# The head of a streaming encoder kernel: order of the first loads and splits, and two sums on another engine

## The reference

```
def _swiglu(u, w_in, w_out):
    h = u @ w_in
    a, b = h[..., :D_FF], h[..., D_FF:]
    return (jax.nn.silu(a) * b) @ w_out

x = x + 0.5 * _swiglu(_rmsnorm(x, norm_ffn1[i]), ffn1_w_in[i], ffn1_w_out[i])
```

## Time and profile before

| | us |
|---|---|
| median of 3 runs | 1879.09 |
| lowest and highest run | 1878.52, 1880.51 |
| profiled execution, its own time | 1879.91 |
| its span, first to last instruction | 1878.1 |
| TensorE busy | 1855.2 (99%) |
| VectorE busy | 1251.5 (67%) |
| ScalarE busy | 866.9 (46%) |
| GpSimd busy | 329.5 (18%) |

### The profile page before, as it was taken

The page is one execution under the profiler, slowest core; times in us unless marked ns, Lnnn a source line. Parts: engine busy times, 40 slices in busy tenths (PEclk is TensorE's granted clock), DMA queues, the critical chain, the costliest instruction groups (busy, mean ns, idle before and its releaser), DMA issues.

```text
span 1878.1 us, 34441 instructions
## 1 busy us (share of the span) xinstructions
PE 1855.2 (99%) x13850; PEld 1834.6 (98%) x13850; DVE 1251.5 (67%) x1999; ACT 866.9 (46%) x1518; POOL 329.5 (18%) x352
## 2 busy tenths in 40 slices
PE   8999999999999999999999999999999999999998
PEld 8999999998999999999999999999989999999998
DVE  7874487668884488679853886563546888548853
ACT  7552355347552355346532553232334665235532
POOL 2220122131220122132201221300010322012112
PEclk9999999999999999999999999999999999999999
DMA  8773576334763576347644763231113576357632
GB/s 207 166 149 105 128 167 148 108 85 95 166 147 108 127 167 150 107 107 165 146 131 102 171 141 101 86 102 68 57 45 103 117 169 152 108 120 167 135 93 82
DMA packets 116830, 234.71 MB, mean 125 GB/s; under 512 B 13184, under 2 KB 15248, under 8 KB 116672
## 3 DMA queue, kind: packets, MB, share of 16 engines
q1 hardware_dynamic: 77440, 160.59, 28.7%
q0 software_dynamic: 38208, 69.42, 22.5%
q10 hardware_dynamic: 1024, 2.49, 0.4%
HBM read 228.92 MB, written 3.53 MB: 124 GB/s over the span
## 4 chain that ended last, share of the span: by engine, by line
PE 93%; DVE 4%; ACT 2%; DMA 1%; issue 1%; DVEq 0%; ACTq 0%
PE ps L1850 49%; PE ps L1840 39%; DVE w_lo L1231 1%; PE ps L1895 1%; PE ps L2167 1%; PE ps L2233 0%; DVE u L1285 0%; DMA raw_z<-in_ffn_in 0%; PE ps L2170 0%; DMA x<-in_x 0%; PE ps L2032 0%; PE ps L2157 0%; DVE rstd L1302 0%; ACT w_hi L726 0%; PE ps L2142 0%
## 5 line engine op out<-in xcount | busy, mean ns | idle before, releaser
L1850 PE MATMUL ps<-u,w_hi 128*128 128x288 f32 x4928 | 984.0, 295 | 11.7 <-DVE w_lo L1231 4.5
L1850 PEld LDWEIGHTS ps<-u,w_hi 128*128 128x128 f32 x4928 | 790.6, 188 | 16.4 <-DVE w_lo L1231 9.4
L1850 PE MATMUL ps<-u,w_lo 128*128 128x288 f32 x2464 | 727.1, 295 | 0.0
L1850 PEld LDWEIGHTS ps<-u,w_lo 128*128 128x128 f32 x2464 | 462.6, 188 | 0.0
L1840 PE MATMUL ps<-h_hi,w_hi 128*128 128x288 f32 x1386 | 294.4, 293 | 0.0
L1840 PE MATMUL ps<-h_lo,w_hi 128*128 128x288 f32 x1386 | 294.3, 293 | 0.0
L1840 PE MATMUL ps<-h_hi,w_lo 128*128 128x288 f32 x1386 | 294.3, 293 | 0.0
L726 ACT ACTIVATE w_hi<-w_raw 128x768 fp32r<-128x768 f32 (+3 forms) x164 | 136.0, 836 | 316.6 <-PE ps L1840 240.2
L1231 DVE TENSOR_TENSOR w_lo<-w_raw,w_hi 128x768 fp32r<-128x768 f32 (+3 forms) x164 | 168.8, 1038 | 160.6 <-ACT w_hi L726 158.4
L1840 PEld LDWEIGHTS ps<-h_hi,w_lo 128*128 128x128 f32 x1386 | 220.4, 188 | 0.0
L1840 PEld LDWEIGHTS ps<-h_hi,w_hi 128*128 128x128 f32 x1386 | 220.3, 188 | 0.0
(11 more groups left out here) (268 smaller groups left out, 2123.5 us busy)
## 6 DMA issues: line engine op xcount, KB each, us to landing
raw_a<-in_ffn_in SPq DMA_DIRECT2D x132, 256.0 KB, 4.2
w_raw<-in_ffn_out SPq DMA_DIRECT2D x64, 384.0 KB, 3.2
raw_y<-in_ffn_in SPq DMA_DIRECT2D x88, 256.0 KB, 3.6
raw_x<-in_ffn_in SPq DMA_DIRECT2D x88, 256.0 KB, 2.7
raw_x<-in_ffn_in POOLq DMA_DIRECT2D x88, 256.0 KB, 6.5
raw_y<-in_ffn_in POOLq DMA_DIRECT2D x88, 256.0 KB, 4.9
raw_z<-in_ffn_in POOLq DMA_DIRECT2D x88, 256.0 KB, 5.1
w_raw<-in_ffn_out SPq DMA_DIRECT2D x64, 320.0 KB, 3.0
```

The lines of the kernel that those rows point to most:

```text
L1850: mm = pe.matmul(dst, w, m, start=prod in ("M1", "M2", "M5") and kp == 0 and p == 0, stop=kp == KP - 1 and p == 2, skip_group_check=prod i ...
```

## The change

Five things change, all at the program's head. SyncE loads A21 of pair 1 ahead of x tile 1. SyncE waits for the landing of S1 of pair 0 before it issues A12, A12 and A22. ScalarE and VectorE split u7's part 0 of tile pair 1 before they read tile pair 2, and M5's block of pair 0 before all odd tiles. S2 of pairs 0 and 1 is made by a GpSimd add (`first_s2`), no longer by VectorE. And since VectorE's add no longer stands behind M5's `w_lo`, SyncE's loads of A21 for pairs 2 and 3 wait for that `w_lo` too.

```
@@ SyncE
                 if g >= 2:
                     sp.wait_ge(s2_summed, g - 1)
+                if 2 <= g < 4:
+                    sp.wait_ge(lo_split, f.unit(ph, "M5", n - 2) + 1)
...
             load_x(6)
+            load_a21(ffn_a, 0, 1)
             load_x(1)
-            load_a21(ffn_a, 0, 1)
...
             load_x(7)
+            sp.wait_ge(s1_summed[0], 16)
             load_ffn(ffn_a, ffn_b)
@@ GpSimd
+            def first_s2(n):
+
+                pool.wait_ge(a11_landed[n], 16)
+                pool.wait_ge(s1_summed[n], 16)
+                pool.tensor_tensor(raw_z[n][:, :], raw_y[n][:, :], raw_x[n][:, :], ALU.add).then_inc(s2_summed, 1)
+
             add_s1_first(ffn_a, 0)
-            add_s3_first(ffn_a, 0)
+            for n in range(2):
+                first_s2(n)
+                add_s3(ffn_a, 0, n)
@@ ScalarE; VectorE has the same moves with u7_low
+            u7_high(ffn_a, 1, 0)
             first_even(2)
-            u7_high(ffn_a, 1, 0)
...
+            upto(ffn_a.unit(0, "M5", 0))
             first_odd(0)
             first_odd(1)
-            upto(ffn_a.unit(0, "M5", 0))
@@ VectorE, in lo(u)
-                if SLOT[u] is None and prod == "M5":
+                if SLOT[u] is None and prod == "M5" and g >= 2:
```

More of the change, by code:

```diff
@@ L1446, in _ @@
             first_even(1)
+            u7_low(ffn_a, 1, 0)
             first_even(2)
-            u7_low(ffn_a, 1, 0)
             first_even(3)
```

## The result

Thirteen runs of each kernel on one chip: before 1878.78 us in the median (1875.51 to 1882.94), changed 1884.47 (1879.88 to 1888.07). The ratio is 1.0025 with a 95% interval of 1.0015 to 1.0034: the changed kernel is 4.7 us slower (2.8 to 6.4). The profiled execution of the changed kernel has a span of 1881.9 us, 1878.1 before. Of all runs told of here one, of the kernel before, was in a slower state (2589.94 us), and it is in no ratio.

What follows compares the result with a forecast made beforehand. TensorE was taken as the bound, with VectorE feeding it at the head; later M5 of pair 1 and slow clock put M2's end at 29.45 against 26.95, 2.5 us on 1879.09: 1881.6 us, range 1877.8 to 1884.2.

Steps and rivals of the forecast that it cites:

- L: Landing of GpSimd's accumulate making raw_x0 (S1 of pair 0): 14.8 us instead of 15.24, with bounds 12.0 and 15.24.
- if L is under 14: Sign for the changed kernel's profile: the forecast is wrong if that accumulate lands before 14 us.
- M1: Even tiles reordered at the head: no gain at M1's end, 14.46 us, and no effect on the clock.
- The first hole: TensorE's idleness before M5 of pair 0: w_lo held by GpSimd's add, start at L + 2.15 = 16.95, 0.7 us sooner.
- The second hole: TensorE idle between M5 of pairs 0 and 1 for 2.2 to 3.5 us, ending at 22.05 against 20.5.
- the second add: GpSimd's add from L + 2.5 to L + 3.8, costing VectorE some 0.9 us; bounds 0 and 1.3.
- The clock: TensorE at 0.50 for 5.9 us after 22.05, so M2 ends at 29.45 against 26.95, 2.5 us later.
- So the 2.5 us go through: From M2's end to the program's end: the 2.5 us delay carries through in full.
- nor does other work end later than TensorE: Premise after M2: M6's third quarter split and its matmul both move by some 2 us.
- rival B: Clock does not fall, or returns at once: -0.1 to +1.3 us, 1879.0 to 1880.4; chance 0.20.
- C: Rival at the head: the accumulate lands early, L = 12.0 to 13.5; 1877.2 to 1878.9 us; chance 0.13.
- D: Rival: held loads free nothing, L stays 15.2, second add costs 1.3; 2.0 to 4.6 us later; chance 0.22.

Runs made afterwards that it cites:

- the repetitions: The changed kernel, unchanged, compared twice more with the kernel before: ratios 1.0014 and 1.0013.
- loads only: The kernel before with only the loads' part: A21 of pair 1 ahead of x tile 1, A12, A12, A22 held back; ratio 1.0003.
- GpSimd's sums only: The kernel before with only S2 of pairs 0 and 1 made by GpSimd adds, loads and order as before; ratio 1.0005.
- swapped and filled: The kernel before with VectorE's M5 w_lo of pair 0 and next sum ahead of kp 1's odd split, plus seven small TensorE products before M5; ratio 1.0015.
- the filled kernel: The changed kernel with ten small unread TensorE products between M5 of pair 0 and M5 of pair 1; ratio 1.0014 to the kernel before.

## Why the prediction was right, and where it was not

**The time.** 2.5 us later was forecast, 4.7 (2.8 to 6.4) came first, 2.6 (0.6 to 4.7) and 2.4 (0.0 to 5.1) in the repetitions. The sign was right, and the size is that of the head in the profiles. By the first ratio more was lost than the head explains; the last section says where such differences can come from.

**L.** Forecast 14.8, measured 13.89, 13.89 and 13.49. The landing took 6.87, 6.46 and 6.64 us from the issue; forecast were 6.9 to 7.0, 0.45 less than before, and 0.5 to 1.1 less than the 7.4 and 7.5 of before came. The issue itself was at 7.02, 7.43 and 6.85, where I had kept 7.84. It is no gift of the change: the other four kernels with the changed loads have it at 6.96 to 8.09, so this is spread that one profile doesn't show. By my own sign, "if L is under 14", this term was wrong in all three, and the prediction came through by the term that cancelled it.

**M1.** Its end was forecast at 14.46, and the clock put at nothing. It ended at 15.16, 14.10 and 14.32: in the first profile the clock was at 0.50 from 11 to 14 us. That cost nothing, since M5's w_lo ended only at 15.86, but a part of the first hole was closed by it and not by M5. It isn't the new order's work: the clock fell in M1 in eight of the 14 profiles, three of them with the even tiles in the old order (loads only, GpSimd's sums only, swapped and filled).

**The first hole.** M5's w_lo was held by GpSimd's add and took 1.29 us (forecast 1.3 to 1.4), and TensorE started at L + 2.03 (forecast L + 2.15). At 15.92 for 16.95, this difference is L's.

**The second hole.** M5 of pair 1 starts at 22.05, the number forecast, by two errors that cancel: L 0.9 sooner, and L + 8.16 for L + 7.25. The term that was mis-sized is the second add, 0.9 with bounds of 0 and 1.3; the held split took 2.53 us for 0.76, 1.8 more. I had the split under way end before the add takes effect. It had begun 0.33 us ahead of the add, and ended 0.61 behind it. So the number 22.05 is luck; what it hangs on, VectorE's w_lo of pair 1 behind a held operation, is as forecast. My upper bound, one whole add of 1.3, left out that the add itself could be longer (1.59) and that the operation had most of its own time still before it when the add was over.

**The clock.** It fell in the second hole and stayed low for 5.8 us after work began, 5.9 forecast, so that M2's end at 29.68 met the 29.45 forecast. In the two others M2 ended 1.1 and 1.5 us sooner. The 5.9 us that I carried over from one row of the profile before were one draw, and that the first profile drew nearly the same was luck: the kernel before itself had 2.9 us in its second profile. The difference between the kernels hangs less on it than each time does: P is 2.73 us later between the two first profiles, 2.81 between the two second ones.

**From M2's end to the end of the program.** "So the 2.5 us go through" held: M2's end is 2.73 us later and so is P, and in all three profiles of the changed kernel TensorE's work is the chain from M5 of pair 1 to about 42 us. The premise, "nor does other work end later than TensorE", was thinner than I had it. I looked at one place, M6's third quarter, where 1.0 us was to spare, and not at how VectorE's list goes on behind it; the room is the 1.3 to 1.7 us that VectorE waits for TensorE. A delay of TensorE goes through in full, a gain only as far as this room. It failed where the prediction counted gains with it, in rival B, that the clock comes back: 1879.0 to 1880.4, a P up to 0.1 us sooner than before and at most 1.3 later. In the filled kernel the clock did come back, M2 ended 2.3 us sooner behind L than in the changed kernel, and P only 0.85: 51.96 is 2.5 us later than the 49.42 of before, 1.9 if its later L is allowed for. The ratio to before, 1.0014, is that of the changed kernel on the same chip, 1.0014.

**The rivals.** C's early landing (12.0 to 13.5) was just met once (13.49), and won nothing: M5 of pair 1 hangs on VectorE. The 4.2 us that I took for the best landing of an accumulate isn't the least in that trace, which has 3.9 (an S3 issued at 211.19); with it C's lower bound of L is 11.7 for 12.0. D fell with its L of 15.2, though its second add, a whole 1.3 us, was nearer to the 1.8 measured than the forecast's 0.9; the loads held back do bring L forward, but only where someone waits for it.

## What to carry to other kernels

Before moving an urgent operation ahead in an engine's list, ask what the engine does in the time that it now waits: here VectorE came to stand for 1.1 to 2.5 us where it had stood for 0.6, and everything behind came late by the difference. Behind a stop of TensorE look for the next point where another engine's list is the limit, and how much room there is: a delay goes through in full, a gain only up to that room. And a sum moved to GpSimd is not off VectorE if operations like w_lo and the splits of u7 stand beside it: here it was relieved of two sums of 0.6 us and stood 2.4 us for them.

## What the runs showed of the hardware

**A held operation that began first.** The Trainium skill ("SBUF — State Buffer", section "SBUF: two separate sides") calls the port pair that VectorE and GpSimd share an exclusive lock, which goes to whichever operation starts first, for the whole instruction. The w_lo rows agree: they began inside an add and ended 0.54 and 0.55 us behind its end (15.32 to 15.86, and 19.18 to 19.73 with the sums alone). The split of u7 in the changed kernel does not quite: it began at 15.90, the add at 16.23, and by the rule the add alone should have waited. The add was 0.3 us longer, and the split still ended 0.61 behind it. The second profile has the same (15.90 for 2.51, add 16.20 for 1.59). In the trace of the kernel before, a split of the same shape that began 0.58 us ahead of an add kept its 0.75, as the rule has it and as I had counted:

```profile
1463.66 0.75 DVE L1285 TENSOR_TENSOR u<-stage,u 128x576 fp32r<-128x576 f32 x1
```

```profile
1464.24 1.47 POOL L673 TENSOR_TENSOR sumsq<-sumsq,sq 128x576 f32<-128x576 f32 x1 [3.55 <-ACT sq L1126]
```

Why the one was held and the other not, no row shows. GpSimd's issue of a DMA, which lay beside the held split too (15.62 for 0.87), doesn't do it by itself: beside that of 18.47 (0.86) in the kernel before, VectorE's operations of 18.09 and 18.76 took their 0.75 and 0.69.

**How long the clock stays low** is not a constant of a kernel: behind the same hole of 4.3 us it was 5.8 us in one execution and 3.3 in the next.

**Two paces at full clock.** A feed-forward block's output stage makes eight tiles of 66 products, and VectorE's adds into x lie either 8.58 or 8.80 us apart, all through a stage. Two stages of one execution of the changed kernel (its third profile), and the same two of the kernel before:

```profile
165.00:215.00 50.00, 50.00 (x377) 50.00 (x376) 16.25 (x21) 9.39 (x13) 1.73 (x2) 1.00 0.31 85
357.00:407.00 50.00, 50.00 (x386) 50.00 (x386) 31.68 (x38) 17.98 (x26) 15.46 (x12) 1.00 0.33 93
```

```profile
164.00:214.00 50.00, 50.00 (x387) 50.00 (x386) 16.56 (x22) 10.36 (x15) 1.73 (x2) 1.00 0.33 88
356.00:406.00 50.00, 50.00 (x378) 50.00 (x377) 30.41 (x37) 16.84 (x24) 15.49 (x12) 1.00 0.32 89
```

At a granted clock of 1.00 in all four, and with TensorE busy throughout, 50 us hold 386 or 387 products, or 377 or 378; 66 in 8.58 or 8.80 us are 0.130 or 0.133 us each. Which stage is slow changes from execution to execution of one kernel: five, three and one of the eight stages in the changed kernel's three profiles, two and two in those of before, at other places. The count goes with what is left of the span behind P: over the 14 profiles, a straight line gives 1824.4 us plus 1.43 for each slow stage, with a scatter of 1.4. Eight slow stages make the two longest spans, 1887.0 and 1887.6. This can be why the 35 runs of one kernel on one chip lie up to 13 us apart, why the unchanged kernel came out at 1.0006 against itself, and why a head that is 2.5 us longer was measured as 4.7 once and as 2.6 and 2.4 later; the runs without a profile don't show their paces. I took it for chance and not for the change's work, since the repeated profiles differ among themselves as much as the kernels do; what sets a stage's pace was not tried.
